# Expert routing of a two-block transformer kernel: logits in the projection stage, wide prefix products, slot lists by one-hot products

## What is computed

```python
def hierarchical_moe(h, w_rg, b_rg, w_re, b_re, w1, w3, w2):      # h: 512 x 1024
    g_prob = softmax(xt @ w_rg + b_rg)                            # 4 groups
    g_idx = argmax(g_prob); g_w = g_prob[g_idx]
    e_logits = (xt @ w_re + b_re).reshape(n_tok, 4, 8)[g_idx]     # the 8 experts of the best group
    top_p, top_i = top_k(softmax(e_logits), 2)
    comb = g_w * top_p / sum(top_p)
    expert = g_idx * 8 + top_i
    ...                                                           # the rows of each expert are gathered
    y = (silu(x_blk @ w1[e]) * (x_blk @ w3[e])) @ w2[e]           # 1024 -> 512 -> 1024
    ...                                                           # and added to their tokens with weight comb
```

## Time and profile before

| | |
|---|---|
| median of the timed runs | 3141.03 us |
| profiled execution | 3143.92 us, its span 3141.7 us |
| busy, TensorE products / weight loads | 2734.3 / 2218.6 us |
| busy, VectorE / ScalarE / GpSimd | 2072.0 / 1327.8 / 760.0 us |
| mean granted TensorE clock | 0.929 of 2.4 GHz |
| memory traffic | 646 MB, mean 206 GB/s |

### The profile page before, as it was taken

The page is one execution under the profiler, slowest core; times in us unless marked ns, Lnnn a source line. Parts: engine busy times, 40 slices in busy tenths (PEclk is TensorE's granted clock), DMA queues, the critical chain, the costliest instruction groups (busy, mean ns, idle before and its releaser), DMA issues. The chain is left out here.

```text
span 3141.7 us, 35888 instructions
## 1 busy us (share of the span) xinstructions
PE 2734.3 (87%) x12794; PEld 2218.6 (71%) x12794; DVE 2072.0 (66%) x3558; ACT 1327.8 (42%) x2049; POOL 760.0 (24%) x559
## 2 busy tenths in 40 slices
PE   4976889799969999999999995986689489999994
PEld 3434668557757999999999984763567478888883
DVE  4334547799957777777777765406523389999994
ACT  2112552115633333333333324234334178887873
POOL 1000023140023433333334322420221122222220
PEclk8978989899989999999999997996889689999997
DMA  7710012234579988888888852220021389999993
GB/s 248 242 57 17 1 56 81 91 127 163 210 273 323 308 283 298 281 287 297 301 292 294 296 190 81 81 84 4 23 86 34 138 316 377 373 370 381 365 365 137
DMA packets 261486, 646.33 MB, mean 206 GB/s; under 512 B 47836, under 2 KB 104924, under 8 KB 260060
## 3 DMA queue, kind: packets, MB, share of 16 engines
q1 hardware_dynamic: 214892, 501.88, 44.5%
q0 software_dynamic: 46448, 142.67, 13.7%
HBM read 614.47 MB, written 55.12 MB: 213 GB/s over the span
## 5 line engine op out<-in xcount | busy, mean ns | idle before, releaser
L2784 ACT ACTIVATE ex_w_hi<-expert_raw 128x1024 fp32r<-128x1024 f32 x384 | 368.2, 1072 | 6.7 <-PE bank L2760 6.7
L1680 PE MATMUL bank<-v_hi,peer_w_hi 128*128 128x512 f32 x768 | 301.8, 393 | 18.3 <-DVE peer_w_lo L1786 18.3
L210 POOL TENSOR_TENSOR w_lo<-ring,w_hi 128x512 fp32r<-128x512 f32 (+1 forms) x136 | 173.1, 1303 | 552.4 <-ACT w_hi L200 552.4
L1680 PE MATMUL bank<-v_lo,peer_w_hi 128*128 128x512 f32 x768 | 301.6, 393 | 0.0
L1680 PE MATMUL bank<-v_hi,peer_w_lo 128*128 128x512 f32 x768 | 301.6, 393 | 0.0
L2830 DVE TENSOR_TENSOR ex_w_lo<-expert_raw,ex_w_hi 128x1024 fp32r<-128x1024 f32 x256 | 296.1, 1219 | 1.4 <-ACT ex_w_hi L2784 0.3
L1668 PE MATMUL bank<-h_hi,u_hi 128*128 128x384 f32 x832 | 278.5, 335 | 1.0 <-DVE u_lo L1747 1.0
L1668 PE MATMUL bank<-h_hi,u_lo 128*128 128x384 f32 x832 | 278.6, 335 | 0.0
L1668 PE MATMUL bank<-h_lo,u_hi 128*128 128x384 f32 x832 | 278.3, 334 | 0.0
L1722 ACT ACTIVATE v_hi<-v_in 128x1024 fp32r<-128x1024 f32 x128 | 130.0, 1054 | 347.3 <-PE bank L1680 325.6
L1655 POOL DMA_INDIRECT got_rows<-in_u_rows,diff x128 | 183.9, 1437 | 313.6 <-DVE got_rows L1754 285.4
(11 more groups left out here) (488 smaller groups left out, 6193.3 us busy)
## 6 DMA issues: line engine op xcount, KB each, us to landing
expert_raw<-in_w SPq DMA_DIRECT2D x384, 512.0 KB, 6.0
v_in<-in_expert_v SPq DMA_DIRECT2D x128, 512.0 KB
u_in<-in_u_tiles SPq DMA_DIRECT2D x104, 512.0 KB, 4.3
ada_in<-in_w_ada SPq DMA_DIRECT2D x48, 512.0 KB, 5.4
gates_by_key<-spread SPq DMA_DIRECT2D x6, 4096.0 KB, 11.6
gate_in<-gates_by_key SPq DMA_DIRECT2D x384, 64.0 KB
ring<-in_w_in SPq DMA_DIRECT2D x11, 2048.0 KB, 8.5
early_u<-in_u_tiles SPq DMA_DIRECT2D x24, 512.0 KB, 3.7
```

The source lines that it names most:

```text
L210: eng.tensor_tensor(g.w_lo[:, k, 0:cols], g.ring[u % RING][:, k, 0:cols], g.w_hi[:, k, 0:cols].bitcast(F32), ALU.subtract).then_inc(s["z_f ...
L1680: last = pe.matmul(g.bank[2 + o][:, :], x[:, par, e, i * P:(i + 1) * P], v[:, par, e, c], start=(first and n == 0), stop=(final and n == 3 ...
L2784: act.activation(hi[kind][:, c, :], raw_piece(raw, u * PIECES + c), ACT.Copy).then_inc(s["r_hi"], 1)
```

## The change

- The logits of tile i are made inside the last `mix_out` call, between products, into banks 0 to 3; the router's weights and biases are loaded at the start of that stage.
- In all three calls of `mix_out` the flips of a tile stand before the sixth chunk of the next group, not after the group; ScalarE writes the flipped tile before the next statistics, and VectorE takes its half before the next sum.
- In `route` the prefix sums are made by VectorE additions over tiles (`earlier`) and three products. `first_slots`, the first 128 rows of each expert, come from eight products of one-hot places with tagged one-hot experts. The weights of the pairs are computed behind them. SP starts the expert loads first and clears the list behind them. The row buffer is cleared here.
- The eight scatters to the list stand in `run_experts`, behind the third gather; SP reads the list back ahead of the loads of expert 7, TensorE flips it after expert 8, VectorE writes `slots`, which only `run_overflow` reads. ScalarE and VectorE split the first weights of expert 0 before its rows.

```diff
@@ Products.pe
+    def pe(self, pe, n, out, between=None):
@@ for k in range(DC):
+            if between is not None:
+                between(k)
             if first:
                 self.wait_low(pe, unit, k)
@@ mix_out
+        def logits(pe, i):
+            if store is None:
+                return
+            if i == 0:
+                pe.wait_ge(s["e_w"], 32)
+            pe.wait_ge(s["f_act"], 4 * (i + 1))
+            pe.wait_ge(s["f_dve"], 4 * (i + 1))
+            for k in range(DC):
+                pe.matmul(g.bank[i][:, 0:RG], g.ht[:, k, i * P:(i + 1) * P], router[:, k, :], start=(k == 0), stop=(k == DC - 1))
...
-                products.pe(pe, n, g.bank[n % 4][:, :])
-                if n > TT:
-                    norm.pe(pe, n - TT - 1)
+                i = n - TT
+
+                def between(k):
+                    if i >= 1 and k == 5:
+                        norm.pe(pe, i - 1)
+                    if i >= 2 and k == 2:
+                        logits(pe, i - 2)
+                products.pe(pe, n, g.bank[n % 4][:, :], between)
+            logits(pe, TT - 2)
             norm.pe(pe, TT - 1)
+            logits(pe, TT - 1)
@@ mix_out, scalar
-            for i in range(TT + 1):
-                if i < TT:
-                    norm.act_stats(act, i)
+            for i in range(TT):
                 if i:
                     norm.act_out(act, i - 1)
+                norm.act_stats(act, i)
+            norm.act_out(act, TT - 1)
@@ mix_out, vector
+                    if u and i:
+                        transposed(dve, i - 1)
@@ route, sync
+                sp.wait_ge(g.rows_stored, 2 * TT * 16)
+                begin(sp)
                 sp.wait_ge(s["q_zero"], 1)
                 sp.dma_start(table.rearrange("(r p) o -> r (p o)", p=P), zero[:, :]).then_inc(s["q_clear"], 16)
-                sp.wait_ge(g.rows_stored, 2 * TT * 16)
-                begin(sp)
-                sp.wait_ge(s["q_sent"], 16 * 2 * TT)
-                sp.dma_start(rows[:, :], table.rearrange("(r p) o -> r (p o)", p=P)).then_inc(s["q_rows"], 16)
+                sp.wait_ge(s["q_clear"], 16)
@@ route, tensor
+                pe.wait_ge(s["q_both"], 1)
+                pe.matmul(g.bank[4][:, 0:TT * NE], before[:, :], flat[0], start=True, stop=False)
+                pe.wait_ge(s["q_earlier"], 1)
+                pe.matmul(g.bank[4][:, 0:TT * NE], g.ones[:, :], flat[1], start=False, stop=True).then_inc(s["q_pos"], 1)
+                pe.matmul(g.bank[5][:, 0:NE], g.ones[:, :], earlier[:, TT, :], start=True, stop=True).then_inc(s["q_pos"], 1)
+                pe.wait_ge(s["q_tagged"], 1)
+                for c in range(2):
+                    pe.wait_ge(s["q_place"], c + 1)
+                    for i in range(TT):
+                        last = pe.matmul(g.bank[6][:, 0:NE], at_place[:, c, i, :], tagged[:, c, i, :],
+                                         start=(c == 0 and i == 0), stop=(c == 1 and i == TT - 1))
@@ route, vector
+                for i in range(TT):
+                    last = dve.tensor_tensor(earlier[:, i + 1, :], earlier[:, i, :], both[:, i, :], ALU.add)
...
+                dve.tensor_tensor(tagged[:], hit[:], tag[:].unsqueeze(3).to_broadcast([P, 2, TT, NE]), ALU.mult).then_inc(s["q_tagged"], 1)
+                dve.wait_ge(s["q_pos"], 1)
+                step(dve.tensor_tensor(prod ... hit ... g.bank[4] ..., ALU.mult))
+                step(dve.tensor_reduce(place[:], prod[:], AX_X, ALU.add))
+                for c in range(2):
+                    dve.tensor_tensor(at_place[:, c], g.iota_p ..., place[:, c, :] ..., ALU.is_equal).then_inc(s["q_place"], 1)
...
+                dve.wait_ge(s["q_list"], 1)
+                step(dve.tensor_scalar(absent[:, :], g.bank[6][:, 0:NE], 0.0, ABSENT, ALU.is_equal, ALU.mult))
+                step(dve.scalar_tensor_tensor(first_slots[:, :], g.bank[6][:, 0:NE], -1.0, absent[:, :], ALU.add, ALU.add))
@@ run_experts, sync
                     load_piece(sp, a, raw, raw_in, q)
+                    if q == PIECES * EXPERT_LOADS.index((LIST_AT - 1, 0)):
+                        sp.wait_ge(s["r_sent"], 16 * 2 * TT)
+                        sp.dma_start(list_rows[:, :], table.rearrange("(r p) o -> r (p o)", p=P)).then_inc(s["r_rows"], 16)
@@ run_experts, gpsimd
-                pool.memset(g.ht[:, 0:4, :], 0.0).then_inc(s["r_zero"], 1)
-                pool.wait_ge(s["r_zero"], 1)
                 for n in range(3):
                     gather(n)
+                pool.iota(pair_i ...); pool.tensor_copy(pair[:, :, :], pair_i[:, :, :])
+                for i in range(TT):
+                    for c in range(2):
+                        pool.indirect_dma_start(out=table, out_offset=... slot[:, c, i:i + 1] ..., in_=pair[:, c, i:i + 1], in_offset=None).then_inc(s["r_sent"], 16)
@@ run_experts, tensor
+                    if n == LIST_AT:
+                        pe.wait_ge(s["r_rows"], 16)
+                        pe.transpose(g.bank[7][:, 0:P], list_rows[:, :], g.ident[:, :]).then_inc(s["r_flip"], 1)
@@ run_experts, scalar and vector
+                weights_hi(0, 0)
                 rows_hi(0)
-                weights_hi(0, 0)
...
+                weights_lo(0, 0)
                 rows_lo(0)
-                weights_lo(0, 0)
```

More of the change, by code:

```diff
@@ L2347, with route @@
 RAW = 3
-def route(g, begin, table, slot, weight, slots, over):
-    nc, a = g.nc, g.a
+def route(g, begin, table, slot, weight, first_slots, over):
+    nc = g.nc
     with ExitStack() as ctx:
@@ L2406, in _ @@
-                pool.wait_ge(s["q_clear"], 16)
-                for i in range(TT):
-                    for c in range(2):
-                        pool.indirect_dma_start(out=table, out_offset=bass.IndirectOffsetOnAxis(ap=slot[:, c, i:i + 1], axis=0),
-                                                in_=pair[:, c, i:i + 1], in_offset=None).then_inc(s["q_sent"], 16)
+                pool.memset(gl[:, :, :], LOW).then_inc(s["q_low"], 1)
+                step(pool.iota(tag_i[:, :, :], pattern=[[T, 2], [P, TT]], base=1, channel_multiplier=1))
@@ L2412, in _ @@
+                pool.tensor_copy(tag[:, :, :], tag_i[:, :, :]).then_inc(s["q_tag"], 1)
+                step(pool.memset(earlier[:, 0, :], 0.0))
+                pool.tensor_tensor(before[:, :], g.causal_t[:, :], g.ident[:, :], ALU.subtract).then_inc(s["q_ready"], 1)
+                pool.memset(zero[:, :], ABSENT).then_inc(s["q_zero"], 1)
+                step(pool.memset(g.ht[:, 0:4, :], 0.0))
             @block.tensor
             def _(pe):
-                pe.wait_ge(s["q_w"], 64)
-                for i in range(TT):
-                    for k in range(DC):
-                        last = pe.matmul(g.bank[0][:, i * 64:i * 64 + RG], g.ht[:, k, i * P:(i + 1) * P], w[:, k, :], start=(k == 0), stop=(k == DC - 1))
@@ L2418, in _ @@
-                last.then_inc(s["q_mm"], 1)
-                pe.wait_ge(s["q_hits"], 1)
-                pe.wait_ge(s["q_ready"], 1)
-                for i in range(TT):
-                    for j in range(i + 1):
-                        pe.matmul(g.bank[1][:, i * NE:(i + 1) * NE], before[:, :] if j == i else g.ones[:, :], both[:, j, :],
-                                  start=(j == 0), stop=(j == i))
-                for j in range(TT):
-                    last = pe.matmul(g.bank[1][:, TT * NE:(TT + 1) * NE], g.ones[:, :], both[:, j, :], start=(j == 0), stop=(j == TT - 1))
@@ L2428, in _ @@
-                last.then_inc(s["q_pos"], 1)
-                pe.wait_ge(s["q_rows"], 16)
-                pe.transpose(g.bank[2][:, 0:P], rows[:, :], g.ident[:, :]).then_inc(s["q_flip"], 1)
+                wide = [both[:, :, :], earlier[:, 0:TT, :]]
+                flat = [v.rearrange("p i e -> p (i e)") for v in wide]
+                pe.wait_ge(s["q_ready"], 1)
+                pe.wait_ge(s["q_both"], 1)
+                pe.matmul(g.bank[4][:, 0:TT * NE], before[:, :], flat[0], start=True, stop=False)
@@ L2432, in _ @@
+                last.then_inc(s["q_list"], 1)
             @block.scalar
@@ L3016, in begin @@
                 load_piece(sp, a, raw, raw_in, q)
-        route(g, begin, table, slot, weight, slots, over)
+        route(g, begin, table, slot, weight, first_slots, over)
         with ExitStack() as local:
-            run_experts(g, raw, raw_in, slots, x_rows, y_rows)
+            run_experts(g, raw, raw_in, slots, first_slots, slot, table, x_rows, y_rows)
             run_overflow(g, over, [raw[0:2]], [raw[2][:, :, :].rearrange("p k n -> p (k n)")], slots, x_rows, y_rows)
```

106 lines of the change are left out of this document (58 added, 48 removed).

## The result

| | before | after |
|---|---|---|
| median of the timed runs | 3141.1 us (5 runs, 3134.0 to 3145.2) | 3126.0 us (5 runs, 3121.4 to 3129.5) |
| ratio after / before | | 0.9948, 95% interval 0.9928 to 0.9969 |
| span of the profiled execution | 3141.7 us | 3124.3 us |
| mean granted clock | 0.929 | 0.935 |

The change makes the kernel 15.1 us faster. 28.3 us were forecast; 3126.0 lies above the range of 3104 to 3124. In the profiled pair the first expert product comes 23.7 us earlier, and of these the expert stage gives 5.0 back.

A forecast was written before the change was run, and what follows sets the result against it. The serial routing chain before the first expert product, then TensorE in the expert stage, was taken as the bound; -33.4 + 3.9 + 1.0 + 0.2 = -28.3 us gave 3113 us, range 3104 to 3124.

The forecast's parts named there:

- First call: First mix_out call: waits for scaled tiles and earlier flips cost net +3.9 us, between +1 and +5.
- Second call: Second mix_out call: nothing is waited for, only the flips add +1.0 us, bounds 0 and 2.3.
- Third call and stage start: Last mix_out call, with flips and logits inside: the routing stage starts at 2464.9 instead of 2458.33.
- VectorE's chain: Routing stage: choice, prefix sums, slot list and weights take 16.1 us, ending at 2481.0 against 2514.32.
- The clear is held by the loads: End of routing: the clear, queued behind twelve expert loads, lands after them, so SP ends the stage at 2485.0.
- rival (a): End of routing: the clear is not held by the loads, VectorE ends the stage at 2481.0; 3110 us, chance 0.18.
- First product at G + 6.8: Head of expert stage: flips 3.36 us after the first gather, product 3.5 later, at 2493.3, a gain of 33.4 us.
- Expert stage, +0.2 for one flip and one copy: Expert stage: only one TensorE flip (0.13 us) and one VectorE copy (0.29 us) are added, 0.2 us.
- Rival (b): Projection groups and routing: waits inside groups and a longer chain cost more than counted, +8 us, 3121; chance 0.2.

The follow-up runs named there:

- e4: Changed kernel with the old order of flips restored in the first two mix_out calls: 3118.9 us, ratio to before 0.9934.
- e3: Changed kernel with the clear of the list issued ahead of the first expert loads: 3120.1 us, ratio to before 0.994.
- e6 to e8: Changed kernel with, in turn, first reload held until first gathered rows land, both engines splitting rows before weights, only VectorE doing so: 3125.2, 3125.8 and 3132.9 us.
- e10 to e14: Kernel before with 64, 512, 256, 128 spare bytes before the transposed intermediates (64, 128 slow; 512, 256 fast), or 64 before the transposed rows (up products 395 ns).

## Why the prediction was wrong

- **First call**, +3.9 forecast: +4.1. The stall before the first tile's flips was 1.88 us (forecast 2.0), the two later 0.61 each (0.7). Right.
- **Second call**, +1.0: +1.0 from its first sum to the next stage; without the new order, in e4, 0.1. Right.
- **Third call and stage start**, 2464.9: 2470.33 less the 5.24 by which this call's fifth sum, the first of the second half, comes later in the profile (2436.66 against 2431.42) is 2465.1. The stall before its first flips was 1.07 us (1.3), and the last sum comes 6.1 us later by this count (5.8); some 0.5 of it, by the estimate above, is the slower pace of the products, which no term had. The last logit block took the 3.52 us of the lower clock level, as assumed. Right within 0.2, in part because the shorter stall and the slower products offset each other.
- **VectorE's chain**, 2481.0: 2487.02 - 5.24 = 2481.8. A product with 128 moving columns was followed by the next one 0.59 us later (both its instructions: 0.80 us), near the narrow bound as taken (0.5). Right within 0.8, and off the path.
- **The clear is held by the loads**: right, and rival (a) wrong; e3 shows 1.5 us ahead of them and 13.3 behind. The Trainium skill, "DMA: Bandwidth & Descriptors", Queues, rings and completion order, has the increment of a DMA land after earlier writes of the same engine; the two landings agree. Its size was short: the loads started 0.95 us later than taken (the last row store took 4.55 us to land, where the median in the earlier trace rows is 3.4), the clear landed 19.7 instead of 18.7 us after the first of them, and the gather started 1.9 instead of 1.5 us after that: G, the start of the first gather, at 2494.03 - 5.24 = 2488.8 instead of 2486.5, +2.3 us.
- **First product at G + 6.8**: the first wrong step, an overlap taken as free. Flips 5.65 instead of 3.36 us after the gather, +2.3; from there 3.38 (forecast 3.5). I had moved work of VectorE and, with it, SyncE's reloads beside the gather and carried over the duration of a gather that had run alone. e6 to e8 show both parts.
- **Expert stage, +0.2 for one flip and one copy**: the second wrong step and the largest, +5.0 measured. I had read that TensorE never waits, which stayed true, and took its product time for a constant. That the change also moves two tiles by 576 bytes was in the diff; that it has a price was in no row. No rival covered it.

Sum: -28.3 + 2.3 + 2.3 + 5.0 = -18.7, against -18.4 at the end of the expert stage and 17.4 us between the two spans. The 0.3 between the first two is that the third call's fifth sum came 5.24 us later, where the forecast had 3.9 + 1.0 for the calls ahead of it. The median, 15.1 us, is less by 3; its interval reaches from 9.7 to 22.6 us, and the drift in the untouched stages explains such a difference but was not traced to a cause. Rival (b), 3121, came nearest in time by another mechanism: its price for longer waits in groups did not appear.

## What to carry to other kernels

When a change allocates or reorders tiles in a stage bound by TensorE, compare the distance between stationary and moving tiles before and after, and read the mean duration of its products, not only its waits. Work that is moved beside a GpSimd gather was not free: VectorE's subtraction of two SBUF tiles cost 0.75 us, the loads beside it 1.5; a later start of the reload (one wait) was worth more than a new order of the splitting. A small transfer that a stage must see landed goes ahead of the large ones.

## What the runs showed of the hardware

- A 128x512 product took 6 to 7 ns longer when its stationary tile lay 64, 128 or 576 bytes past a multiple of 1024 from the moving tile, and not at 0, 256 or 512. The projections agree: 0.227 us between two starts at multiples of 256 bytes, 0.233 at 64 past one, 0.232 at 128. Why is open. The Trainium skill, "TensorE: Matmul & The Clock Gate", Step-by-step: what each phase is for, says that loading the next weights takes no SBUF read bandwidth from the running product; by that rule the distance would not be expected to matter, and the measurement (e10 to e14) decides: it does. Whether two reads compete is not shown.
- What GpSimd does for one gather grew by 0.75 us beside VectorE's splitting, and by nothing beside ScalarE's.
